# A mixture-of-experts loop whose last two items share one schedule: gate and up products of both first, then the down products of both

## What is computed

```
gu  = xb @ w_gu[e] + b_gu[e]                    # 1024 -> 2048
gt  = minimum(gu[:, :1024], 7); up = clip(gu[:, 1024:], -7, 7)
act = (up + 1) * gt * sigmoid(1.702 * gt)
y   = act @ w_dn[e] + b_dn[e]                   # 1024 -> 1024
out = segment_sum(y_sorted * gate, tok_sorted)  # back to the tokens
```

## Time and profile before

| | |
|---|---|
| three timed runs | 1569.92, 1576.63, 1577.48 us (median 1576.63) |
| the profiled execution | 1570.03 us, its span 1568.2 us |
| PE busy | 1501.6 us (96%) |
| DVE, ACT busy | 486.5 us (31%), 332.1 us (21%) |
| HBM traffic over the span | 345 GB/s mean, 428 to 429 GB/s in the expert layer |
| granted TensorE clock, mean | 0.992 |

### The profile page before, as it was taken

The page is one execution under the profiler, slowest core; times in us unless marked ns, Lnnn a source line. Parts: engine busy times, 40 slices in busy tenths (PEclk is TensorE's granted clock), DMA queues, the critical chain, the costliest instruction groups (busy, mean ns, idle before and its releaser), DMA issues.

```text
span 1568.2 us, 24420 instructions
## 1 busy us (share of the span) xinstructions
PE 1501.6 (96%) x9769; PEld 786.0 (50%) x9769; DVE 486.5 (31%) x1134; ACT 332.1 (21%) x791; POOL 6.8 (0%) x13
## 2 busy tenths in 40 slices
PE   6999899999999999999999999999999999999996
PEld 5788885776577686433333333333333333333333
DVE  2666566323301024323222232132212321321324
ACT  2333551223312102111112111111111111111113
POOL 0000000000000000000000000000000000000000
PEclk9999999999999999999999999999999999999999
DMA  9848443534499975799999999999999999999994
GB/s 393 346 159 351 199 164 121 224 125 150 140 326 367 345 298 216 284 425 427 428 428 428 428 429 428 428 429 428 429 429 428 428 428 429 428 429 428 428 428 180
DMA packets 60167, 541.39 MB, mean 345 GB/s; under 512 B 7202, under 2 KB 11810, under 8 KB 29506
## 3 DMA queue, kind: packets, MB, share of 16 engines
q1 hardware_dynamic: 59378, 534.65, 82.8%
q0 software_dynamic: 720, 5.76, 0.9%
HBM read 533.54 MB, written 6.84 MB: 345 GB/s over the span
## 4 chain that ended last, share of the span: by engine, by line
PE 75%; DMA 15%; DVE 7%; issue 2%; ACT 1%; SPq 0%; ACTq 0%; DVEq 0%
PE banks L572 22%; DMA ring<-w_gu 13%; PE banks L618 12%; PE banks L1378 9%; PE banks L921 5%; PE banks L552 4%; PE banks L1203 2%; DMA ring<-wpre 2%; DVE regA L728 2%; PE banks L1135 2%; PE banks L589 2%; PE banks L1019 2%; PE banks L840 1%; PE banks L1228 1%; DVE regA L726 1%
## 5 line engine op out<-in xcount | busy, mean ns | idle before, releaser
L572 PE MATMUL banks<-ring,regA 128*64 128x512 f32 x1536 | 342.4, 594 | 6.6 <-DMA ring<-w_gu 6.6
L572 PEld LDWEIGHTS banks<-ring,regA 128*64 128x64 f32 x1536 | 107.7, 137 | 221.4 <-issue 205.3
L701 DVE TENSOR_TENSOR regB<-regB,banks 128x528 f32<-128x528 f32 x128 | 81.5, 699 | 327.6 <-PE banks L552 327.6
L618 PE MATMUL banks<-ring,regC 128*64 128x512 f32 x768 | 170.1, 595 | 1.2
L667 ACT ACTIVATE regA<-regA 128x512 f32<-128x512 f32 x32 | 20.2, 630 | 524.3 <-DVE regA L723 524.3
L723 DVE TENSOR_SCALAR regA<-banks 128x512 f32<-128x512 f32 x32 | 22.1, 692 | 342.0 <-PE banks L589 342.0
L618 PEld LDWEIGHTS banks<-ring,regC 128*64 128x64 f32 x768 | 54.3, 137 | 101.5 <-issue 95.7
L527 PE MATMUL banks<-regC,regA 128*64 128x512 f32 (+1 forms) x396 | 99.2, 619 | 1.0 <-DVE regA L693 1.0
L921 PE MATMUL banks<-low,ring 128*128 128x264 f32 x320 | 72.2, 387 | 0.9 <-ACT regC L1620 0.9
L552 PE MATMUL banks<-regA,regC 64*128 64x264 f32 x512 | 71.6, 409 | 0.0
L921 PEld LDWEIGHTS banks<-low,ring 128*128 128x128 f32 x320 | 60.5, 190 | 12.1 <-issue 1.8
(11 more groups left out here) (519 smaller groups left out, 1757.3 us busy)
## 6 DMA issues: line engine op xcount, KB each, us to landing
ring<-w_gu SPq DMA_DIRECT2D x96, 2048.0 KB, 25.6
ring<-w_dn SPq DMA_DIRECT2D x48, 2048.0 KB, 27.6
ring<-wpre SPq DMA_DIRECT2D x41, 2048.0 KB, 13.4
regC<-w_gu SPq DMA_DIRECT2D x16, 2048.0 KB, 25.3
low<-w_gu SPq DMA_DIRECT2D x16, 2048.0 KB, 25.6
ring<-kvT SPq DMA_DIRECT2D x64, 256.0 KB, 4.7
ring<-kv SPq DMA_DIRECT2D x64, 256.0 KB, 6.2
regC<-w_dn SPq DMA_DIRECT2D x8, 2048.0 KB, 29.0
```

The lines of the kernel that those rows point to most:

```text
L572: mm = pe_mm(bank[x // 2][SLOT * (x % 2):SLOT * (x % 2 + 1), :], lhsT=hg[:, k % 4, SLOT * (k // 4):SLOT * (k // 4 + 1)], rhs=weights_k[:, ...
L618: mm = pe_mm(bank[5][SLOT * y:SLOT * (y + 1), :], lhsT=actT[:, m % 4, SLOT * (m // 4):SLOT * (m // 4 + 1)], rhs=slots[s][:, D * (m % 4) + ...
L701: V.tensor_tensor(pair, pair, banks[:, b:b + 2, 0:T], ALU.add).then_inc(acc_added, 1)
```

## The change

Items 30 and 31 get one common schedule. PE: gate and up products of item 30; the steps between as before; gate, up and bias products of item 31; down products of item 30; turning item 31's activation; the scatter of item 30's result, in banks 6, 2, 6, 2; the first half of item 31's down products; turning its selection; the gather of the next item's tokens and turning them; the second half of the down products. SP issues the weights in the order in which PE now reads them: gate and up of 30, gate and up of 31, down of 30, down of 31. ACT leaves its loop after 30 items and DVE after 31; the rest is written out in the new order. Further items run as before. In the cut diff below, `item` for PE calls `gate_up`, `middle` and `down` with the instructions of before.

```diff
--- before.py
+++ after.py
         SCATTER_BANKS = (6, 2, 4, 6)
+        LATE_BANKS = (6, 2, 6, 2)
         LAST_BANKS = (0, 2, 4, 0)
...
-
-        def for_items(eng, first, item):
-
-            with eng.Fori(first, NE) as j:
-                item(j)
-            K = number_of_items(eng)
-            with eng.If(K > NE):
-                with eng.Fori(NE, NJ) as j:
-                    with eng.If(j < K):
-                        item(j)
-            return K
...
@@ -508,10 +498,12 @@
-            for j in range(NE - 2, NE):
-                for c in range(6):
-                    sp.wait_ge(moe_read, 6 * j + c - SLOTS + 1)
-                    load(c, j, (6 * j + c) % SLOTS)
+            n = 6 * (NE - 2)
+            for j, cs in ((NE - 2, range(4)), (NE - 1, range(4)), (NE - 2, (4, 5)), (NE - 1, (4, 5))):
+                for c in cs:
+                    sp.wait_ge(moe_read, n - SLOTS + 1)
+                    load(c, j, n % SLOTS)
+                    n += 1
...
@@ -539,14 +531,14 @@
-            def scatter(at):
+            def scatter(at, homes=SCATTER_BANKS):
 
                 pe.wait_ge(ytok_copied, at(1, 1))
                 pe.wait_ge(selT_copied, at(1, 1))
                 for q in range(4):
-                    b = SCATTER_BANKS[q]
-                    if q == 3:
-                        pe.wait_ge(acc_added, at(4, 2))
+                    b = homes[q]
+                    if b in homes[:q]:
+                        pe.wait_ge(acc_added, at(4, 2 + homes.index(b)))
...
+            def gate_up(at, homes, first=False, late=False):
+                    if c == (1 if first else 0) and not late:
-                pe.wait_ge(acc_added, at(4, 5))
+                if not late:
+                    pe.wait_ge(acc_added, at(4, 5))
...
                                rhs=brow[NE * u:NE * (u + 1), HALF * y:HALF * (y + 1)], start=False, stop=True, skip_group_check=True)
                     if y == 1:
                         mm.then_inc(gu_ready, 1)
+
+            def gather_next():
                 gather_tile(2, GROW, True)
                 gather_prompt()
 
+            def turn_selection(at):
                 pe.wait_ge(selg_new, at(1, 1))
                 for i in range(2):
                     pe.transpose(bank[6][:, P * i:P * (i + 1)], selg[:, i, :, :].rearrange("p a s -> p (a s)"), ident)
                 pe_mm(bank[6][:, NPR:T], lhsT=selg[:, 2, :, :].rearrange("p a s -> p (a s)"),
                       rhs=ident[:, SROW], start=True, stop=True).then_inc(selT_turned, 1)
-                pe.wait_ge(gtok_copied, at(1, 2))
-                turn_gathered(0, 2)
+
+            def turn_products(at, homes=(4, 2)):
                 pe.wait_ge(act_ready, at(1, 1))
                 for y in range(2):
                     for q in (2 * y, 2 * y + 1):
-                        mm = pe.transpose(bank[4 - 2 * y][:, P * q:P * (q + 1)], act_[:, P * q:P * (q + 1)], ident)
+                        mm = pe.transpose(bank[homes[y]][:, P * q:P * (q + 1)], act_[:, P * q:P * (q + 1)], ident)
                     mm.then_inc(a_turned, 1)
-                turn_gathered(2, 4).then_inc(g_turned, 1)
-                for m in range(8):
+
+            def down(at, homes, first, last):
+                for m in range(first, last):
                     s, landed = homes[4 + m // 4]
                     if m % 4 == 0:
                         pe.wait_ge(slot_in[s], landed)
@@ -621,9 +618,43 @@
                     if m % 4 == 3:
                         mm.then_inc(moe_read, 1)
 
+            def middle(at):
+                gather_next()
+                turn_selection(at)
+                pe.wait_ge(gtok_copied, at(1, 2))
+                turn_gathered(0, 2)
+                turn_products(at)
+                turn_gathered(2, 4).then_inc(g_turned, 1)
+
+            def item(at, homes, first=False):
...
+                down(at, homes, 0, 8)
+
+            def homes_of(places):
+                return [(i % SLOTS, moe_base[i % SLOTS] + 16 * (i // SLOTS + 1)) for i in places]
+
+            def last_two():
+                j = NE - 2
+                n = 6 * j
+                one, two = (lambda m, a: m * j + a), (lambda m, a: m * (j + 1) + a)
+                homes = homes_of((n, n + 1, n + 2, n + 3, n + 8, n + 9)), homes_of((n + 4, n + 5, n + 6, n + 7, n + 10, n + 11))
+                gate_up(one, homes[0])
+                middle(one)
+                gate_up(two, homes[1], late=True)
+                down(one, homes[0], 0, 8)
+                turn_products(two, (4, 0))
+                scatter(two, LATE_BANKS)
+                down(two, homes[1], 0, 4)
+                pe.wait_ge(acc_added, two(4, 5))
+                turn_selection(two)
+                gather_next()
+                pe.wait_ge(gtok_copied, two(1, 2))
+                turn_gathered(0, 4).then_inc(g_turned, 1)
+                down(two, homes[1], 4, 8)
+
...
@@ -638,8 +669,7 @@
-            fixed(NE - 2)
-            fixed(NE - 1)
+            last_two()
...
@@ -678,7 +708,45 @@
-            for_items(act, 0, item)
+            def last_two():
+                j = NE - 2
+                act.wait_ge(gmin_ready, j + 1)
+                A(sgm[:, :], gmn[:, :], ACT.Sigmoid, scale=1.702).then_inc(sig_ready, 1)
+                act.wait_ge(gathered, j + 2)
+                A(gtok[:, :], bank[2][:, :], ACT.Copy).then_inc(gtok_copied, 1)
+                act.wait_ge(selT_turned, j + 1)
+                A(selT[:, :], bank[6][:, 0:T], ACT.Copy).then_inc(selT_copied, 1)
+                for y in range(2):
+                    act.wait_ge(a_turned, j * 2 + (y + 1))
+                    A(actT[:, 2 * y:2 * y + 2, :], bank[4 - 2 * y][:, 256 * y:256 * (y + 1)].rearrange("p (q s) -> p q s", q=2),
+                      ACT.Copy).then_inc(actT_ready, 1)
+                act.wait_ge(g_turned, j + 2)
+                A(hg[:, :, :], bank[3][:, :].rearrange("p (q s) -> p q s", q=4), ACT.Copy).then_inc(hg_ready, 1)
+                act.wait_ge(gmin_ready, j + 2)
+                A(sgm[:, :], gmn[:, :], ACT.Sigmoid, scale=1.702).then_inc(sig_ready, 1)
+                act.wait_ge(moe_read, 6 * NE - 2)
+                A(ytok[:, :], bank[5][:, :], ACT.Copy).then_inc(ytok_copied, 1)
+                for y in range(2):
+                    act.wait_ge(a_turned, (j + 1) * 2 + (y + 1))
+                    A(actT[:, 2 * y:2 * y + 2, :], bank[4 - 4 * y][:, 256 * y:256 * (y + 1)].rearrange("p (q s) -> p q s", q=2),
+                      ACT.Copy).then_inc(actT_ready, 1)
+                act.wait_ge(selT_turned, j + 2)
+                A(selT[:, :], bank[6][:, 0:T], ACT.Copy).then_inc(selT_copied, 1)
+                act.wait_ge(gathered, j + 3)
+                A(gtok[:, :], bank[2][:, :], ACT.Copy).then_inc(gtok_copied, 1)
+                act.wait_ge(g_turned, j + 3)
+                A(hg[:, :, :], bank[3][:, :].rearrange("p (q s) -> p q s", q=4), ACT.Copy).then_inc(hg_ready, 1)
+                act.wait_ge(moe_read, 6 * NE)
+                A(ytok[:, :], bank[5][:, :], ACT.Copy).then_inc(ytok_copied, 1)
+
+            with act.Fori(0, NE - 2) as j:
+                item(j)
+            last_two()
+            K = number_of_items(act)
+            with act.If(K > NE):
+                with act.Fori(NE, NJ) as j:
+                    with act.If(j < K):
+                        item(j)
...
@@ -710,15 +778,19 @@
+                def weigh():
+                    dve.wait_ge(selT_copied, j + 1)
+                    for i, r in tok_tiles:
+                        ins = V.tensor_scalar(selg[r, i, :, :], iota[r, :].unsqueeze(1).to_broadcast([r.stop - r.start, 2, SLOT]),
+                                              rr[r, i, bass.ds(j, 1)], gg[r, i, bass.ds(j, 1)], ALU.is_equal, ALU.mult)
+                    ins.then_inc(selg_new, 1)
+
                 dve.wait_ge(gathered, j + 1)
                 V.tensor_scalar(pick[0:2 * NE, :], ones[0:2 * NE, 0:SLOT], owner[0:2 * NE, bass.ds(j, 1)], None, ALU.mult)
                 choose(bass.ds(j + 1, 1)).then_inc(sel_new, 1)
-                dve.wait_ge(selT_copied, j + 1)
-                for i, r in tok_tiles:
-                    ins = V.tensor_scalar(selg[r, i, :, :], iota[r, :].unsqueeze(1).to_broadcast([r.stop - r.start, 2, SLOT]),
-                                          rr[r, i, bass.ds(j, 1)], gg[r, i, bass.ds(j, 1)], ALU.is_equal, ALU.mult)
-                ins.then_inc(selg_new, 1)
-                add(j)
+                weigh()
+                if not late:
+                    add(j)
                 dve.wait_ge(gu_ready, j * 2 + 1)
                 V.tensor_scalar(gmn[:, :], bank[0][:, :], 7.0, None, ALU.min).then_inc(gmin_ready, 1)
                 dve.wait_ge(gu_ready, j * 2 + 2)
@@ -727,9 +799,18 @@
                 dve.wait_ge(sig_ready, j + 1)
                 V.tensor_tensor(act_[:, :].rearrange("p (q n) -> p n q", q=4), upc[:, :].rearrange("p (n q) -> p n q", q=4),
```

(30 more changed lines are left out.)

## The result

| | runs | median us | lowest to highest |
|---|---|---|---|
| before | 20 | 1571.57 | 1568.97 to 1577.48 |
| changed | 20 | 1577.08 | 1570.40 to 1579.61 |

The ratio of the changed kernel to the one before is 1.0029, interval 1.0019 to 1.0038: 3.0 to 6.0 us slower, within the half percent. The forecast was 2.7 us slower.

What follows compares the result with a forecast made beforehand. The prediction took DMA as the bound up to 1535.05 and PE after it. PE's steps after 1535.1 summed to 18.64 us against 15.95, so 2.7 us added to the median gave 1579.3 us, range 1570 to 1583.

Steps and rivals of the forecast that it cites:

- The transfers: Weight loads of items 30 and 31: every chunk lands when it does now, cost 0.
- Up to the landing: PE before 1535.1: item 31's products start at 1515.3, and PE has caught up with the DMA at 1535.1, as now.
- The sum: PE's steps from 1535.1 to the last down product's end: 18.64 us against 15.95, so 2.69 later.
- half product with ytok copy: After 1535.1, second half of item 30's down product, 3.63 us, plus 0.68 to the scatter's start: 4.31.
- gather and gtok copy: Next item's gather, now alone between products, 2.60 us (bounds 1.9 to 3.0), then 0.77 for the gtok copy.
- The scatter's two waits: In the late scatter, product groups 2 and 3 wait for DVE's adds 0 and 1: 2.77 us instead of 2.17.
- The activation chain leaves the path: Item 31's activation, 4.2 us from its bias products, is hidden under item 30's down product.
- Level: Whole-kernel time: timed runs seen at two levels, the median at the upper; 2.7 us added to it gives 1579.3.
- the end does not follow the last landing: Rival at the end: only the last half down product follows the landing of 1544.9; 2.5 us sooner, 1574.1; chance 0.10.
- The steps do not cancel: Rival at the end: scatter and gather waits come out low, nothing to be seen, within 1 us of 1576.6; chance 0.17.
- No engine stalls on a fetch behind its loop: Rival at DVE's and ACT's loop exits: an instruction fetch queues like a weight chunk, 33.5 us, giving 1595.5; chance 0.05.
- The clock stays at 1.00 from 1535 to 1560: Rival after 1535.1: PE's clock falls to 1.2 GHz, adding up to 15 us, 1594; chance 0.02.

Runs made afterwards that it cites:

- the written out kernel: Kernel before, with ACT's items 30 and 31 and DVE's item 31 written out behind the loops in the old order; ratio 1.0001 to the kernel before.
- early gather: Changed kernel with the next gather beside item 31's bias products, its transposes between halves of item 30's down product; ratio 0.9986 to the kernel before.

## Why the prediction was right, and where it was off

- *The transfers*: 0 forecast, 0 found. The interval between the two awaited landings is the same to 0.01 us, and issues come in the old rhythm.
- *Up to the landing*: forecast start of item 31's products 0.8 us behind the end of item 30's middle: they show 0.80 of idle, and PE has caught up with place 9 with 1.24 us of waiting (1.4 forecast).
- *The sum*: 18.64 forecast from 1535.1 to the last product's end, 19.1 found (1540.17 to 1559.26). By its terms, forecast and found: half product with ytok copy 4.31 and 4.36; scatter 2.77 and 2.78; first half 3.46 and 3.58; selection 0.50 and 0.49; gather and gtok copy 3.37 and 3.65; transposes 0.60 and 0.58; last half 3.63 and 3.65. The direction and the list of steps held. The term that missed most is the gather: I had 12 records at 0.216 and 0.77 for the copy, and the rows show 2.94 and a gap of 0.70. The high bound for it, 3.0, was the better value; that weight loads cause it, as I put there, no run tested. The rows do show that the gather's price depends on its neighbours. Beside the bias products it adds 1.9 us to them (20 records in 2.90 us from 1538.68 to 1541.58, the eight bias records alone 1.05 in the changed kernel from 1534.23 to 1535.28), and alone it takes 2.94: moving it out of their company cost about 1 us by itself.
- *The scatter's two waits* at 0.60: shown, 0.61 go with them.
- *The activation chain leaves the path*: shown by the order of rows, DVE done by 1538.5 against a use at 1543.76. Not separately priced by a run.
- *Level*: I put 2.7 us on a median of 1576.63 from three runs; twenty have 1571.57. So the start was 5.1 us too high, while the two medians lie 5.5 us apart and not 2.7. That 1579.3 came within 2.2 us of the measured 1577.08 is luck: two errors of opposite sign. The step itself is better judged by the interval's centre, 4.55 us, which is 1.9 above the forecast. Of this 0.5 stand in S (3.15 for 2.69) and 0.25 outside the span. The remaining 1.1 us lie within the interval; falls of the clock are large enough for them, but no run shows that they are it. The two levels that I read out of four times are none: with 65 runs the times fill the space between.
- *Rivals*: the end does not follow the last landing (place 11 would land at 1550.0, PE comes to it at 1555.6). The steps do not cancel. No engine stalls on a fetch behind its loop (ACT and DVE wait there for DVE and PE, not on issue), and the written out kernel has the same S. The clock stays at 1.00 from 1535 to 1560. Of its rival the condition ("It needs a long empty stretch on PE") was half right: behind such a stretch the clock did fall, in the kernel before without its gather, but it also falls where there is none (last section). The price was too high: 1.7 us for one fall, and not a doubled remainder.

## What to carry to other kernels

When a wait is removed from a path, list what lay in its shadow: that work must find other cover, or it is the new cost. Here the wait for the chain of DVE and ACT (4.3 us) went. Selection, gather and copy, which had stood beside it, and the scatter, which had stood behind late landings, came out at more: 0.5, 3.65 and 2.8 us. And before taking hidden work off PE, look at what will stand in its place: in the one place tried here, 2.68 us of empty PE cost 1.7 us of clock, while the useless gather had cost nothing.

## What the runs showed of the hardware

- Leaving out the gather and its transposes, 16 records that PE had worked off in the shadow of another wait, made S of the kernel before 1.7 us longer, in both profiles taken, by one fall of the granted clock behind 2.68 us of idle PE (5.35 us for 3.65). The ratio of the times is 1.0015 (1.0000 to 1.0029). Waits of 1.24 us in the changed kernel were followed by none.
- The same stands at the start of the program. Behind a wait of 2.82 us (changed kernel) or 2.84 us (early gather) the next 32 products take 9.08 and 9.07 us; in the other nine profiles the wait is at most 1.38 us and they take 7.36 to 7.39. The Trainium skill, "TensorE: Matmul & The Clock Gate", section "HAM oscillation — how this bites in real kernels", tells of such falls where PE waits for DMA between bursts of products. This case agrees, for a wait for DMA (2.82 us) and for one for DVE (2.68 us).
- The length of one idle stretch does not decide it alone. In all eleven profiles the clock falls between 600 and 640 us, where PE runs small products and then idles for 0.82 to 0.96 us. The gather behind that, twelve records as in item 31, takes 4.59 to 5.58 us there, and 2.94 at a clock of 1.00. The kernel before (PE's row, then the stretch ahead of it and its own):

```profile
621.99 5.12 PE L527 MATMUL banks<-regC,regA 9*64 9x512 f32 x12 [0.95 <-DVE regA L693]
...
620.00:621.99 1.99, 1.04 (x15) 0.78 (x14) 1.20 (x7) 1.92 (x4) 0.00 (x0) 1.00 1.00 428
621.99:627.04 5.05, 5.05 (x12) 0.97 (x12) 1.60 (x8) 0.00 (x0) 0.00 (x0) 0.55 0.98 419
```

- Executions of one kernel differ by up to 10 us, mostly with their mean clock, at 1.05 us per 0.001. In the profiles the falls lie in the first 640 us, and from there to item 31 the clock is at 1.00 in all of them. For changes of a few microseconds the stretch of a profile from one awaited landing to a fixed point told more (15.99 twice, 19.13 and 19.14, 14.90 and 14.91, 17.66 and 17.67) than 12 timed runs.
- ACT's table loads (1.28 us each) at the Sigmoid fell from 32 to 30 with the last two items written out: in a loop each pass loads the table anew, the copies written out behind it need none. None of them stands in the chain that ended last.
- All kernels with written out items have 0.2 to 0.4 us more outside the span than the kernel before.
